# Where an S5 mixer's state coefficients are applied: to B before the scans, or to C between them

## The chip, the cores and the metric

The kernel runs on one core of a Trainium2 chip. The metric is the device time of one execution in microseconds. Three executions of the kernel before gave 1158.82, 1159.68 and 1162.73 us, a median of 1159.68 us.

## The reference

One decoder block over 256 tokens of width 1024, in float32. Cut to what matters here:

```python
h = modulate(rms_norm(x, g_mix), sh1, sc1)
u, q, k, v, ga, gb = split(h @ w_in)
# S5: 32 groups of 16 channels, 64 complex states per group
abar = exp(a * dt);  coef = (abar - 1) / a            # complex, one per group and state
bu   = einsum('bsgc,gpc->bsgp', u, coef[..., None] * b)   # bbar = coef * b
x_   = scan over positions: x_[t] = abar * x_[t-1] + bu[t]
y    = Re(einsum('gcp,bsgp->bsgc', c, x_)) + d_skip * u
y_a  = glu(gelu(y));  y_b = attention(q, k, v) @ w_attn_o     # 8 heads, causal, partial rotary
x    = x + gt1 * ((sigmoid(ga) * y_a + sigmoid(gb) * y_b) @ w_out)
h2   = modulate(rms_norm(x, g_ffn), sh2, sc2)
x    = x + gt2 * moe(h2)          # top 4 of 32 experts, each [1024 x 2048] and [1024 x 1024]
out  = rms_norm(x, g_final)
```

The coefficient `coef` of a state multiplies the state's input. The recurrence is linear, so the same factor may stand on the way out instead: Re(c · (coef · x')) = Re((c · coef) · x'), where x' is the scan of b·u without the coefficient.

## The kernel before, in words

Five engines run one program each, tied by semaphores. The order of each engine's work is written out by hand; no scheduler moves it. A first part (to about 250 us) computes the mixer, with the weights streamed from HBM through `ring`, 12 slots of 1 MB; the rest loops over the 32 experts, 12 MB of weights each, through four regions that the mixer has left (`zone` and `ring`). SyncE (SP) issues nearly all the loads in one order; `wait_free` and the waits on `w_used` hold a load back until TensorE has finished with the slot that it overwrites.

States are laid out as 16 columns of 128 (two groups of 64 states each). The eight *pairs* j cover two columns each. The steps of the S5 part are:

- The *phase tables* `ecos`, `esin` (cosine and sine of t times each state's angle) are built by doubling: VectorE (DVE) for the lower eight columns, GpSimd (POOL) for the upper eight (`square`, `double`, L320 to L325). The recurrence then runs on turned numbers and needs real scans only.
- *B*: `b_in` holds the 16 columns of B. DVE multiplies them by the coefficients (`sprm` 3 and 4, L1549 to L1551), ScalarE (ACT) spreads them into blocks with a mask (L1268, behind the negation of C's imaginary half, L1264), TensorE (PE) transposes the blocks (`b_columns`, L703), and ACT copies the result to `BT` (L1272).
- `b_u(j)` on PE (L678): four products of B with u for pair j, into PSUM banks 4 and 5. For j > 0 it waits until the scans of pair j-1 are done, since all pairs use the same two banks.
- `recurrence(j)` on DVE: six products and sums with the phase tables (L1585 to L1592) and four scans (L1597). Pair 0 to 7 in order.
- POOL turns the scans of pair j back, six operations of 128x512 (L1425 to L1430), into `xs`. All their operands lie in SBUF. From j = 2 on it waits for `xs_read`, the product `c_x(j/2 - 1)`.
- `c_x(m)` on PE (L693) multiplies C with four columns (two pairs) of `xs`; `skip(m)` on DVE (L1618) adds d·u.

These steps are interleaved with the projections (`proj`, L659 and L662) and with the attention of a pair of heads. The loop over p = 0 to 3 stands on PE as: `scores(p)` (L730, L734), first half of `proj(4+p)`, `c_x(p)`, `b_u(2p+3)`, a quarter of the projection, `probs_columns(p)` (L742), the last quarter, `weigh(p)` (L753), `b_u(2p+4)`. On DVE it stands as: `largest(p)` (L1604, waits for the scores), `recurrence(2p+2)`, `inverse_sums(p)`, `skip(p)`, `recurrence(2p+3)`. So `b_u(2p+3)` waits for `recurrence(2p+2)`, which stands behind `largest(p)`, which waits for `scores(p)`. Ahead of the loop DVE does `recurrence(0)`, `rotary(1)` (L1561 to L1564, all in SBUF), `recurrence(1)`.

After the loop come the attention's output projection (L830), the GLU products (L847), the output projection (L922, L949), the router, and the first expert. ACT asks for the router's and the biases' weights (L1284 to L1288, five loads in small packets) just ahead of the GELU (L1290) and two sigmoids (L1293, L1294).

## Time and profile before

| | |
|---|---|
| Median of three executions | 1159.68 us |
| The profiled execution's own time | 1159.92 us |
| Its span, first to last instruction | 1158.0 us |
| PE busy | 1122.6 us (97%) |
| DVE, ACT, POOL busy | 442.8, 140.9, 105.1 us |
| Granted TensorE clock, mean | 0.998 of full speed |
| Moved by DMA | 459.46 MB, mean 397 GB/s |

The span is cut into 40 slices of 29 us in the page's second part, a digit each for the busy share in tenths. Almost every slice has both PE and the DMA engines near full, so neither total says which of them sets the end in which stretch; the chain of waits and the stretches' own DMA shares do. POOL works only in the first five slices, where the S5 part lies. A busy figure of PE contains matmuls whose ends are modelled.

### The profile page before, as it was taken

How to read it: one execution, taken by the hardware profiler on the slowest of the kernel's cores; microseconds unless marked ns; L12 is line 12 of the kernel's file. 1: busy time of each engine (PE TensorE's matmuls, PEld its weight loads, DVE VectorE, ACT ScalarE, POOL GpSimd, SP SyncE). 2: the span in 40 equal slices, each digit the busy share in tenths (PEclk: the TensorE clock that was granted, in tenths of full speed). 3: DMA queues.
4: the chain of work that ended last, by engine and by line, in shares of the span. 5: the costliest groups of instructions: out<-in, count | busy, mean ns of one | idle time of the engine just before them, and what ended most of it. 6: DMA issues, size and time to landing. Idle time of an engine off the chain costs nothing.

```text
span 1158.0 us, 17087 instructions
## 1 busy us (share of the span) xinstructions
PE 1122.6 (97%) x6970; PEld 491.0 (42%) x6970; DVE 442.8 (38%) x952; ACT 140.9 (12%) x313; POOL 105.1 (9%) x142
## 2 busy tenths in 40 slices
PE   8999999999999999999999999999999999999996
PEld 6657788544333333333333333333333333333332
DVE  7857668263222333332222322222222222222224
ACT  3222240231000000000000000000000000000002
POOL 6496810000000000000000000000000000000000
PEclk9999999999999999999999999999999999999999
DMA  9983389999999999999999999999999999999994
GB/s 385 393 305 102 101 335 400 421 349 422 423 427 434 428 428 430 431 430 430 430 434 429 429 432 430 431 425 431 431 430 431 430 431 432 431 431 426 427 424 202
DMA packets 39839, 459.46 MB, mean 397 GB/s; under 512 B 3732, under 2 KB 4248, under 8 KB 16120
## 3 DMA queue, kind: packets, MB, share of 16 engines
q1 hardware_dynamic: 39088, 458.09, 94.3%
q10 hardware_dynamic: 712, 0.81, 0.2%
q8 instruction: 30, 0.49, 0.2%
q14 instruction: 9, 0.07, 0.0%
HBM read 457.83 MB, written 1.05 MB: 396 GB/s over the span
## 4 chain that ended last, share of the span: by engine, by line
PE 78%; DMA 18%; DVE 1%; ACT 1%; issue 1%; SPq 1%; DVEq 0%
PE ps L1086 30%; PE ps L1133 17%; DMA ring<-in_w_gu 16%; PE ps L662 5%; PE ps L1054 4%; PE ps L998 3%; PE ps L847 2%; PE ps L659 2%; PE ps L1110 2%; PE ps L865 2%; DMA ring<-in_first 1%; PE ps L830 1%; PE ps L922 1%; PE ps L623 1%; PE ps L629 1%; PE ps L1118 1%
## 5 line engine op out<-in xcount | busy, mean ns | idle before, releaser
L1086 PE MATMUL ps<-ring,zone 128*64 128x512 f32 x1024 | 227.0, 595 | 9.6 <-DMA ring<-in_w_gu 9.6
L1133 PE MATMUL ps<-ring,tmp 128*64 128x512 f32 x1012 | 224.2, 594 | 10.4 <-ACT tmp L1363 10.4
L1086 PE MATMUL ps<-zone 128*64 128x512 f32 x1024 | 227.2, 595 | 1.3 <-DMA zone<-in_w_gu 1.2
L1854 DVE TENSOR_TENSOR x_tok<-x_tok,ps 128x512 f32<-128x512 f32 x128 | 81.9, 681 | 261.4 <-PE ps L1054 260.1
L1086 PEld LDWEIGHTS ps<-ring,zone 128*64 128x64 f32 x1024 | 70.7, 137 | 161.6 <-issue 143.5
L1133 PEld LDWEIGHTS ps<-ring,tmp 128*64 128x64 f32 x1012 | 83.2, 137 | 130.7 <-issue 130.7
L1086 PEld LDWEIGHTS ps<-zone 128*64 128x64 f32 x1024 | 70.7, 137 | 154.1 <-issue 146.9
L1360 ACT ACTIVATE tmp<-hT 128x256 f32<-128x256 f32 x64 | 23.9, 417 | 722.8 <-DVE hT L1869 722.8
L1869 DVE TENSOR_SCALAR hT<-ps 128x256 f32<-128x256 f32 x64 | 24.2, 419 | 189.9 <-PE ps L1086 189.9
L1848 DVE TENSOR_TENSOR tmp<-ps,zone 128x512 f32<-128x512 f32 x32 | 22.1, 691 | 162.8 <-PE ps L1133 162.8
L1054 PE MATMUL ps<-tmp,xn_tok 64*128 64x512 f32 x248 | 70.0, 641 | 0.0
L662 PE MATMUL ps<-hT,ring 128*128 128x256 f32 x256 | 57.9, 382 | 0.0
L998 PEld LDWEIGHTS ps<-ptmp,zone 128*128 128x128 bf16 x1488 | 45.1, 98 | 23.6 <-issue 23.6
L662 PEld LDWEIGHTS ps<-hT,ring 128*128 128x128 f32 x256 | 47.7, 190 | 7.4 <-issue 1.4
L998 PE MATMUL ps<-ptmp,zone 128*128 128x64 bf16 x1488 | 48.8, 193 | 0.0
L1054 PEld LDWEIGHTS ps<-tmp,xn_tok 64*128 64x128 f32 x248 | 18.7, 184 | 50.3 <-issue 50.3
L865 PE MATMUL ps<-cst,ptmp 32*64 32x512 f32 x256 | 34.8, 613 | 0.0
L1041 PE MATMUL ps<-cst,ptmp 32*64 32x512 f32 x128 | 34.4, 613 | 0.0
L1110 PE MATMUL ps<-cst,ptmp 32*64 32x512 f32 x128 | 34.4, 613 | 0.0
L1363 ACT COPY tmp<-ps 128x256 f32<-128x256 f32 x64 | 20.8, 375 | 86.3 <-PE ps L1118 86.3
L659 PE MATMUL ps<-ring,hT 128*128 128x512 f32 x64 | 28.2, 594 | 0.0
L847 PE MATMUL ps<-zone,ring 128*128 128x256 f32 x128 | 28.2, 380 | 0.0
(339 smaller groups left out, 889.5 us busy)
## 6 DMA issues: line engine op xcount, KB each, us to landing
ring<-in_w_down SPq DMA_DIRECT2D x60, 2048.0 KB, 17.8
zone<-in_w_gu SPq DMA_DIRECT2D x23, 4096.0 KB, 26.9
ring<-in_w_gu SPq DMA_DIRECT2D x23, 4096.0 KB, 29.2
zone<-in_w_gu SPq DMA_DIRECT2D x14, 2048.0 KB, 13.1
ring<-in_w_gu SPq DMA_DIRECT2D x13, 2048.0 KB, 14.1
ring<-in_w_ada SPq DMA_DIRECT2D x16, 1024.0 KB, 13.1
ring<-in_w_in SPq DMA_DIRECT2D x12, 1024.0 KB, 14.6
ring<-in_w_gu SPq DMA_DIRECT2D x10, 1024.0 KB, 9.5
```

Of the source, the lines that this page charges most:

```text
L659: last = mm(ps[:, b + i, :], hT[:, k, P * i:P * i + P], w[:, kk, :], start=(k == 0), stop=(k == KD - 1))
L662: last = mm(ps[:, b + m // 2, (m % 2) * T:(m % 2) * T + T], w[:, kk, P * m:P * m + P], hT[:, k, :], start=(k == 0 and m % 2 == 0), stop=(k ...
L847: last = mm(ps[:, b + m // 2, (m % 2) * T:(m % 2) * T + T], w[:, kk, P * m:P * m + P], gluT[:, kk, :], start=(kk == 0 and m % 2 == 0), sto ...
L865: mm(ps[CAP * h:CAP * h + CAP, b, :], hotb[own, :], brow[own, 512 * h:512 * h + 512], start=True, stop=False, skip_group_check=True)
L998: last = mm(ps[:, 2, CAP * f:CAP * f + CAP], xpart[:, c, i, stored(f)], pick[:, i, :], start=(i == 0 and c == 0), stop=(i == TT - 1 and c ...
L1041: last = mm(ps[CAP * h:CAP * h + CAP, 5, :], hotb[3 * EXPERTS:P, :], brow[3 * EXPERTS:P, 0:2 * T], start=True, stop=True, skip_group_check ...
L1054: mm(ps[:, 6 + h, :], pickwT[half, P * t:P * t + P], ysb[half, :], start=True, stop=True).then_inc(S["comb_up"], 1)
L1086: last = mm(ps[CAP * h:CAP * h + CAP, b, :], hg[:, 2 * j + kk, :], w[:, kk, D * b + 512 * h:D * b + 512 * h + 512], start=False, stop=(j = ...
L1110: last = mm(ps[CAP * h:CAP * h + CAP, 3, :], hotb[own, :], brow[own, 512 * h:512 * h + 512], start=True, stop=False, skip_group_check=True)
L1133: last = mm(ps[CAP * h:CAP * h + CAP, 3, :], actT[:, q, j, :], row[:, 512 * h:512 * h + 512], start=False, stop=(j == DN_PIECES - 1 and q ...
L1854: V.tensor_tensor(x_tok[:, t, 512 * h:512 * h + 512], x_tok[:, t, 512 * h:512 * h + 512], ps[:, bank + h, :], ALU.add).then_inc(S["comb_ad ...
L1869: V.tensor_scalar(rows_of(gate[:, pair[g]]), down_pair(ps[:, 0, :], g), LIMIT, None, ALU.min).then_inc(S["gated"], 1)
```

## The change

B is no longer multiplied by the coefficients. The host lays B out in the transposed blocks, zeros included (512 KB instead of 256 KB), and one load brings them straight into `BT`. DVE's six operations on B, ACT's four spreads, PE's eight transposes and ACT's copy are gone. `weighted_c(m)` is new on DVE: six operations of 128x128 that multiply C's part m, in place, by the coefficients, with the negation of the imaginary half in the last one. Piece 0 stands behind `recurrence(1)`, pieces 1 to 3 behind `recurrence(3)`, `(5)` and `(7)`; `c_x(m)` waits for its piece. `b_u(0, 1)` does two pairs in one go, pair 1 into banks 6 and 7. The five late loads on ACT's queue are issued behind the GELU and the sigmoids.

```diff
--- before.py
+++ after.py
@@ -111,7 +111,12 @@
 
 def b_layout(b_re, b_im):
 
-    return np.concatenate([b[0].reshape(ST, 2, N, C).transpose(1, 2, 0, 3).reshape(P, ST * C) for b in (b_re, b_im)], axis=1)
+    out = np.zeros((4, 2, C, 2, KW, 2, N), np.float32)
+    for r, w in enumerate((b_re, b_im)):
+        w = w[0].reshape(KW, 4, 2, N, C)
+        for q in range(2):
+            out[:, q, :, r, :, q, :] = w[:, :, q].transpose(1, 3, 0, 2)
+    return out.reshape(P, 2 * KW * P)
 
 
 def c_layout(c_re, c_im):
@@ -218,18 +223,11 @@
     def stored(k):
         return slice(P * (2 * (k % RUN) + k // RUN), P * (2 * (k % RUN) + k // RUN) + P)
 
-    def b_sum(r):
-        return tmp[:, r, 0:T].rearrange("p (s c) -> p s c", s=ST)
-
-    b_in = kT.rearrange("p m t -> p (m t)")[:, 0:512].rearrange("p (r s c) -> p r s c", r=2, s=ST)
     work = gbT.rearrange("p m t -> p (m t)")[:, 0:10 * ST].rearrange("p (j s) -> p j s", s=ST)
     sprm = sb("sprm", [P, 5, ST])
 
     def state(j):
         return sprm[:, j, :] if j < 5 else work[:, j - 5, :]
-
-    blk = z.rearrange("p b r n -> p (b r n)")
-    Bblk = blk[:, 0:1024].rearrange("p (r s q c) -> p r s q c", r=2, s=ST, q=2)
 
     wide = 2048
     phases_at, mixer_at = (zone[:, 4 * wide * j:4 * wide * j + 4 * wide] for j in range(2))
@@ -374,6 +371,7 @@
 
     PROJ_BANK = (0, 2, 0, 2, 0, 0, 0, 4)
     TURN_BANK = (2, 0)
+    BU_BANK = (4, 6, 4, 4, 4, 4, 4, 4)
     MOD_BANK = {1: 6, 2: 2}
     LAST_BANK = (6, 0)
     GU_PIECES, DN_PIECES = 4, 2
@@ -459,7 +457,7 @@
             for n in range(place["uq", 3] + 1):
                 load_piece(n)
             sp.dma_start(cst[:, 0:C_ALL], const[:, :]).then_inc(S["const_in"], 16)
-            sp.dma_start(b_in.rearrange("p r s c -> p (r s c)"), b_laid[:, :]).then_inc(S["const_in"], 16)
+            sp.dma_start(BT.rearrange("p r m n -> p (r m n)"), b_laid[:, :]).then_inc(S["const_in"], 16)
             sp.dma_start(CT.rearrange("p r m n -> p (r m n)"), c_laid[:, :]).then_inc(S["const_in"], 16)
             for n in range(place["uq", 3] + 1, place["glu", 0]):
                 load_piece(n)
@@ -664,28 +662,27 @@
                 if part[-1] == 3 and ms[-1] == 3:
                     last.then_inc(w_used, 1)
 
-            def b_u(j):
-
-                if j == 0:
+            def b_u(*pairs):
+
+                if pairs[0] == 0:
                     pe.wait_ge(S["proj_sb"], 1)
-                    pe.wait_ge(S["BT_sb"], 1)
+                    pe.wait_ge(S["const_in"], 48)
                 else:
-                    pe.wait_ge(S["scanned"], 4 * j)
+                    pe.wait_ge(S["scanned"], 4 * pairs[0])
                 for r in range(2):
-                    for q in range(2):
-                        s = 2 * j + q
-                        a = 32 * (s % 4)
-                        last = mm(ps[:, 4 + q, T * r:T * r + T], BT[a:a + 32, r, s // 4, :], uT[a:a + 32, s // 4, :],
-                                  start=True, stop=True, skip_group_check=True)
-                last.then_inc(S["bu_up"], 1)
+                    for j in pairs:
+                        for q in range(2):
+                            s = 2 * j + q
+                            a = 32 * (s % 4)
+                            last = mm(ps[:, BU_BANK[j] + q, T * r:T * r + T], BT[a:a + 32, r, s // 4, :], uT[a:a + 32, s // 4, :],
+                                      start=True, stop=True, skip_group_check=True)
+                last.then_inc(S["bu_up"], len(pairs))
 
             def c_x(m):
 
                 pe.wait_ge(S["xs_set"], 2 * m + 2)
-                if m == 0:
-                    pe.wait_ge(S["const_in"], 48)
-                    pe.wait_ge(S["c_set"], 1)
-                else:
+                pe.wait_ge(S["c_set"], 2 * m + 2)
+                if m > 0:
                     pe.wait_ge(S["y_skip"], m)
                 for r in range(2):
                     for s in range(4):
@@ -693,16 +690,6 @@
                         last = mm(ps[a:a + 32, 6, (m % 2) * T:(m % 2) * T + T], CT[:, r, m, a:a + 32],
                                   xs[:, s // 2, r, T * (s % 2):T * (s % 2) + T], start=(r == 0), stop=(r == 1), skip_group_check=True)
                 last.then_inc(S["xs_read"], 1)
-
-            def b_columns():
-
-                pe.wait_ge(S["mod1_sb"], 4)
-                for r in range(2):
-                    pe.wait_ge(S["Bblk_set"], 2 * r + 2)
-                    for m in range(KW):
-                        last = nc.tensor.transpose(ps[:, 6 + r, P * m:P * m + P],
-                                                   Bblk[:, r, 4 * m:4 * m + 4].rearrange("p s q c -> p (s q c)"), ident)
-                last.then_inc(S["BT_up"], 1)
 
             def turned_columns(n):
 
@@ -767,13 +754,11 @@
             pair(0, 6), pair(0, 7)
             pair(1, 6), pair(1, 7)
             proj(2, 0)
-            b_columns()
             turned_columns(0)
             proj(2, 1, (0,))
-            b_u(0)
+            b_u(0, 1)
             proj(2, 1, (1, 2, 3))
             proj(3, 0)
-            b_u(1)
             turned_columns(1)
             proj(3, 1)
             for p in range(HEADS // 2):
@@ -1260,16 +1245,7 @@
                 nc.scalar.copy(oT[:, p, :], ps[:, 7, 0:T]).then_inc(S["o_sb"], 1)
 
             projected(0, uT)
-            act.wait_ge(S["const_in"], 48)
-            nc.scalar.activation(CT[:, 1], CT[:, 1], ACT.Copy, scale=-1.0).then_inc(S["c_set"], 1)
-            for r in range(2):
-                act.wait_ge(S["Bsum_set"], r + 1)
-                for q in range(2):
-                    nc.scalar.activation(Bblk[:, r, :, q, :], b_sum(r), ACT.Copy,
-                                         scale=cst[:, C_MB + q:C_MB + q + 1]).then_inc(S["Bblk_set"], 1)
             projected(1, q_tok)
-            act.wait_ge(S["BT_up"], 1)
-            nc.scalar.copy(BT[:, :, :, :].rearrange("p r m n -> p (r m n)"), ps[:, 6:8, :].rearrange("p b n -> p (b n)")).then_inc(S["BT_sb"], 1)
             turned(0)
             projected(2, k_tok)
             turned(1)
@@ -1281,17 +1257,17 @@
             head_pair(3)
             head_out(3)
             projected(7, gbT[:, 4:8, :])
+            act.wait_ge(S["y_skip"], KW)
+            nc.scalar.activation(gluT, uT, ACT.Gelu_apprx_tanh).then_inc(S["gelu"], 1)
+
+            act.wait_ge(S["proj_sb"], 8)
+            nc.scalar.activation(gbT, gbT, ACT.Sigmoid).then_inc(S["sig_gb"], 1)
+            nc.scalar.activation(gaT, gaT, ACT.Sigmoid).then_inc(S["sig_ga"], 1)
             act.dma_start(wr.rearrange("p (a b) e -> p a (b e)", b=RUN), w_router[0].rearrange("(a p b) e -> p a (b e)", p=P, b=RUN)).then_inc(S["late_in"], 16)
             act.dma_start(brt[:, :], b_router.to_broadcast([P, EXPERTS])).then_inc(S["late_in"], 16)
             for j in range(2):
                 act.dma_start(brow[EXPERTS * j:EXPERTS * j + EXPERTS, :], b_gu[0, :, D * j:D * j + D]).then_inc(S["late_in"], 16)
             act.dma_start(brow[2 * EXPERTS:3 * EXPERTS, :], b_down[0]).then_inc(S["late_in"], 16)
-            act.wait_ge(S["y_skip"], KW)
-            nc.scalar.activation(gluT, uT, ACT.Gelu_apprx_tanh).then_inc(S["gelu"], 1)
-
-            act.wait_ge(S["proj_sb"], 8)
-            nc.scalar.activation(gbT, gbT, ACT.Sigmoid).then_inc(S["sig_gb"], 1)
-            nc.scalar.activation(gaT, gaT, ACT.Sigmoid).then_inc(S["sig_ga"], 1)
 
             def row_copy(n):
 
@@ -1541,15 +1517,21 @@
                 level(n)
             square(V, link, T // 2, LOW)
 
-            dve.wait_ge(S["const_in"], 48)
-            cr = sprm[:, 3, :].unsqueeze(2).to_broadcast([P, ST, C])
-            ci = sprm[:, 4, :].unsqueeze(2).to_broadcast([P, ST, C])
-            t0, t1 = (tmp[:, j, T:2 * T].rearrange("p (s c) -> p s c", s=ST) for j in range(2))
-            for r in range(2):
-                link(V.tensor_tensor(t0, b_in[:, r], cr, ALU.mult))
-                link(V.tensor_tensor(t1, b_in[:, 1 - r], ci, ALU.mult))
-                V.tensor_tensor(b_sum(r), t0, t1, ALU.subtract if r == 0 else ALU.add).then_inc(S["Bsum_set"], 1)
-                dve.wait_ge(S["Bsum_set"], r + 1)
+            def weighted_c(m):
+
+                if m == 0:
+                    dve.wait_ge(S["const_in"], 48)
+                cr, ci = (sprm[:, j, 4 * m:4 * m + 4].unsqueeze(2).to_broadcast([P, 4, 2 * C]) for j in (3, 4))
+                c0, c1 = (CT[:, r, m].rearrange("p (s c) -> p s c", s=4) for r in range(2))
+                t0, t1 = (tmp[:, r, 0:P].rearrange("p (s c) -> p s c", s=4) for r in range(2))
+                link(V.tensor_tensor(t0, c1, ci, ALU.mult))
+                link(V.tensor_tensor(t1, c0, ci, ALU.mult))
+                link(V.tensor_tensor(c0, c0, cr, ALU.mult))
+                link(V.tensor_tensor(c1, c1, cr, ALU.mult))
+                V.tensor_tensor(c0, c0, t0, ALU.subtract).then_inc(S["c_set"], 1)
+                V.scalar_tensor_tensor(c1, t1, -1.0, c1, ALU.mult, ALU.subtract).then_inc(S["c_set"], 1)
+                dve.wait_ge(S["c_set"], 2 * m + 2)
+
             def rotary(n):
 
                 heads = (q_tok, k_tok)[n].rearrange("p i (h d) -> p i h d", d=HD)[:, :, :, 0:2 * HALF]
@@ -1565,7 +1547,7 @@
                 dve.wait_ge(S["rotated"], n + 1)
 
             double(V, link, T // 2, slice(0, ST // 4), (ptmp, probs))
-            dve.wait_ge(S["Bblk_set"], 4)
+            dve.wait_ge(S["const_in"], 48)
             rotary(0)
             double(V, link, T // 2, slice(ST // 4, ST // 2), (ptmp, probs))
             V.engine_nop().then_inc(S["phases"], 1)
@@ -1574,7 +1556,7 @@
 
                 b = j % 2
                 cs, sn = ecos[:, 2 * j:2 * j + 2, :], esin[:, 2 * j:2 * j + 2, :]
-                br, bi = (ps[:, 4:6, T * r:T * r + T] for r in range(2))
+                br, bi = (ps[:, BU_BANK[j]:BU_BANK[j] + 2, T * r:T * r + T] for r in range(2))
                 t0, t1 = (tmp[:, r, :].rearrange("p (s t) -> p s t", s=2) for r in range(2))
                 zz = [z[:, b, r, :].rearrange("p (s t) -> p s t", s=2) for r in range(2)]
                 dve.wait_ge(S["bu_up"], j + 1)
@@ -1647,6 +1629,7 @@
             recurrence(0)
             rotary(1)
             recurrence(1)
+            weighted_c(0)
             for p in range(HEADS // 2):
                 largest(p)
                 if 2 * p + 2 < 8:
@@ -1655,6 +1638,7 @@
                 skip(p)
                 if 2 * p + 3 < 8:
                     recurrence(2 * p + 3)
+                    weighted_c(p + 1)
 
             def attended(h):
```

Left out above are the two lines that name semaphores. Where the rows of an engine's program move is seen best on DVE, at the start of the loop. Before, behind `rotary(1)` (L1561 to L1564):

```order
L1564 TENSOR_TENSOR zone<-zone,tmp 128x16x16
L1585 TENSOR_TENSOR tmp<-ps,zone 128x512
L1586 TENSOR_TENSOR tmp<-ps,zone 128x512
L1588 TENSOR_TENSOR ps<-ps,zone 128x2x256
L1589 TENSOR_TENSOR ps<-ps,zone 128x2x256
L1591 TENSOR_TENSOR ps<-tmp,ps 128x2x256
L1592 TENSOR_TENSOR ps<-tmp,ps 128x2x256
L1597 SCALAR_TENSOR_TENSOR zone<-sprm,ps 128x256 x4
L1604 TENSOR_REDUCE mx<-ps 128x2
```

The last row is `largest(0)`. After, the same place, from the scans of `recurrence(1)` on:

```order
L1579 SCALAR_TENSOR_TENSOR zone<-sprm,ps 128x256 x4
L1527 TENSOR_TENSOR tmp<-zone,sprm 128x128
L1528 TENSOR_TENSOR tmp<-zone,sprm 128x128
L1529 TENSOR_TENSOR zone<-zone,sprm 128x128
L1530 TENSOR_TENSOR zone<-zone,sprm 128x128
L1531 TENSOR_TENSOR zone<-zone,tmp 128x128
L1532 SCALAR_TENSOR_TENSOR zone<-tmp,zone 128x128
L1586 TENSOR_REDUCE mx<-ps 128x2
```

Six rows now stand between the scans and the reduction; the same six stand at three further places. On PE, before, from the first half of `proj(2)` (L659) on, with `b_columns` (L703), `turned_columns` (L714) and `b_u` (L678):

```order
L659 MATMUL ps<-ring,hT 128x512 x8
L703 MATMUL ps<-head,zone 128x128 x8
L714 MATMUL ps<-head,zone 128x128 x8
L659 MATMUL ps<-ring,hT 128x512 x2
L678 MATMUL ps<-zone 128x256 x4
L659 MATMUL ps<-ring,hT 128x512 x14
L678 MATMUL ps<-zone 128x256 x4
L714 MATMUL ps<-head,zone 128x128 x8
```

After, where L701 is `turned_columns` and L677 is `b_u`:

```order
L657 MATMUL ps<-ring,hT 128x512 x8
L701 MATMUL ps<-head,zone 128x128 x8
L657 MATMUL ps<-ring,hT 128x512 x2
L677 MATMUL ps<-zone 128x256 x8
L657 MATMUL ps<-ring,hT 128x512 x14
L701 MATMUL ps<-head,zone 128x128 x8
```

The eight transposes are gone, and the four products of pair 1 stand with those of pair 0.

## Rows read from the trace of the kernel before

**Rows 1.** PE's waits from 60 to 252 us: total, times, longest.
```profile
PE ps L960 <- DVE zone L1764: 0.2, 1, 0.2
PE ps L1086 <- DVE zone L1787: 0.2, 1, 0.2
```
**Rows 2.** Stretches: length; PE, PEld, DVE, ACT, POOL busy; clock, DMA share, GB/s.
```profile
160.00:226.00 66.00, 65.90 (x301) 48.59 (x301) 41.89 (x31) 14.22 (x15) 0.00 (x0) 1.00 1.01 403
231.00:235.00 4.00, 4.00 (x24) 1.77 (x20) 3.11 (x11) 0.00 (x0) 0.00 (x0) 1.00 0.62 199
300.00:820.00 520.00, 513.97 (x3198) 186.04 (x3196) 149.99 (x346) 33.91 (x90) 0.00 (x0) 1.00 1.01 430
820.00:1129.00 309.00, 294.64 (x1860) 107.16 (x1858) 89.05 (x208) 20.72 (x55) 0.00 (x0) 1.00 1.00 429
```
**Rows 3.** The chain that ended last: start, length, what.
```profile
824.36 7.10 PE ps L1133 x32
...
832.82 36.13 DMA ring<-in_w_gu
```
**Rows 4.** PE's timeline: start, us, line, op, output<-inputs, shape, count.
```profile
50.70 7.03 PE L659 MATMUL ps<-ring,hT 128*128 128x512 f32 x16
57.57 1.04 PE L703 MATMUL ps<-head,zone 128*128 128x128 f32 x8
58.44 1.04 PE L714 MATMUL ps<-head,zone 128*128 128x128 f32 x8
...
113.65 1.13 PE L678 MATMUL ps<-zone 32*128 32x256 f32 x8
...
151.26 1.07 PE L693 MATMUL ps<-zone 128*32 128x256 f32 x16
```
**Rows 5.** DVE's timeline: largest(0); then from the scans of pair 3 to those of pair 4.
```profile
85.87 0.42 DVE L1604 TENSOR_REDUCE mx<-ps 128x2 f32<-128x256 f32 x1 [3.95 <-PE ps L734]
...
98.77 2.41 DVE L1597 TENSOR_TENSOR_SCAN zone<-sprm,ps 128x256 f32<-128x256 f32 x4
105.71 0.42 DVE L1604 TENSOR_REDUCE mx<-ps 128x2 f32<-128x256 f32 x1 [4.53 <-PE ps L734]
...
107.34 0.68 DVE L1585 TENSOR_TENSOR tmp<-ps,zone 128x512 f32<-128x512 f32 x1
...
111.18 2.41 DVE L1597 TENSOR_TENSOR_SCAN zone<-sprm,ps 128x256 f32<-128x256 f32 x4
```
**Rows 6.** DVE's timeline: rotary(1), four operations.
```profile
68.69 0.29 DVE L1561 TENSOR_TENSOR tmp<-zone,cst 128x128 f32<-128x128 f32 x1
69.02 1.02 DVE L1562 TENSOR_TENSOR tmp<-zone,cst 128x128 f32<-128x128 f32 x1
70.07 1.22 DVE L1563 TENSOR_TENSOR zone<-zone,cst 128x256 f32<-128x256 f32 x1
71.32 1.36 DVE L1564 TENSOR_TENSOR zone<-zone,tmp 128x256 f32<-128x256 f32 x1
```
**Rows 7.** POOL's timeline: the tables beside rotary(1), then pairs 0, 2, 3 and 7.
```profile
68.85 1.04 POOL L323 TENSOR_TENSOR zone<-zone 128x508 f32<-128x508 f32 x1
...
71.09 1.32 POOL L325 TENSOR_TENSOR zone<-zone 128x508 f32<-128x508 f32 x1
...
79.79 1.26 POOL L1430 TENSOR_TENSOR zone<-zone,ptmp 128x512 f32<-128x512 f32 x1
...
94.00 1.27 POOL L1425 TENSOR_TENSOR zone<-zone 128x512 f32<-128x512 f32 x1 [3.93 <-PE ps L693]
...
102.10 1.27 POOL L1425 TENSOR_TENSOR zone<-zone 128x512 f32<-128x512 f32 x1
...
148.58 1.27 POOL L1430 TENSOR_TENSOR zone<-zone,ptmp 128x512 f32<-128x512 f32 x1
```
**Rows 8.** ACT's timeline: the first row behind the late loads.
```profile
163.37 1.28 ACT L1290 ACT_TABLE_LOAD   x1 [1.14 <-issue]
```

**Rows 9.** Load issued from 15 to 19 us: queue, count, size, us to landing.
```profile
ring<-in_w_in SPq DMA_DIRECT2D x1, 1024.0 KB, 26.2
```

More of the change, by code:

```diff
@@ L279, in build @@
     shift_set = sem("shift_set")
-    names = """x_in const_in head_in late_in gfin_in out_stored ones_set cond_set sprm_sb Bblk_set
-        BT_up BT_sb c_set phases modrow_sb modT_up mod1_sb sq1 xn1 xT_up
+    names = """x_in const_in head_in late_in gfin_in out_stored ones_set cond_set sprm_sb c_set phases modrow_sb modT_up mod1_sb sq1 xn1 xT_up
         hD_sb hA_sb proj_sb bu_up scanned xs_set xs_read rotated turned_up turned_sb sc_up negmax expd probs
@@ L288, in build @@
         x_split scale1_set turn turned row_max sqsum2 lnD lnA lnP
-        cond_half u_up biased_scale ada_used Bsum_set mask_set phase_hi scale2_set hgl_up hgl_sb sums_set""".split()
+        cond_half u_up biased_scale ada_used mask_set phase_hi scale2_set hgl_up hgl_sb sums_set""".split()
     S = {n: sem(n) for n in names}
```

## The prediction

> **What bounds the kernel now.** I read the chain of waits first. Up to 824 us it is TensorE's own products with a few tenths of a microsecond between them; behind that it steps on to the weight loads [rows 3]. The DMA engines are full in both stretches, 430 and 429 GB/s at a share of 1.01 and 1.00 [rows 2]: from about 256 us on one saturated stream carries the experts' weights, and TensorE first works ahead of its end and is then caught by it. So the end moves with the moment at which that stream starts. What starts it is TensorE: from 160 to 226 us the loads run at 403 GB/s, but from 231 to 235 us they fall to 199 (share 0.62) [rows 2], because every load that may be issued has landed and the next waits for slots that TensorE frees. Whatever was gained or lost in loading before that is forgotten there. TensorE in turn waits 0.4 us in all between 60 and 252 us [rows 1]. The conclusion for the sum: a microsecond more or less on TensorE between 50 and 230 us is a microsecond at the end, and the DMA side gives nothing back.
>
> The second reading is of who is nearly late for TensorE. In the loop over head pairs the DVE idles only ahead of `largest`: 3.95 us in round 0, 4.53 us in round 1, until the scores arrive [rows 5]; round 2 repeats round 1 instruction by instruction, and I count it as equal. From there it has no air. The scans of pair 4 end at 111.18 + 2.41 = 113.59 us [rows 5], and `b_u(5)`, which waits for them, starts at 113.65 us [rows 4]. TensorE and DVE run neck and neck, with a slack that I put at 0.1 us. Any time by which `largest` starts late beyond that is a stall of TensorE at `b_u(2p+3)`.
>
> **The change part by part.** The sum is made against the profiled execution, 1159.92 us (span 1158.0), which lies 0.24 us above the median of 1159.68.
>
> *Transposes gone.* The eight of `b_columns` hold TensorE from 57.57 to 58.44 us, where the next begins [rows 4]: -0.87 us, all on the path.
>
> *DVE's, ACT's work on B gone, BT's copy gone.* These end before `rotary(0)`, which waits for q's projection, and TensorE is in an unbroken product from 50.70 us on until the transposes [rows 4]. Nothing waits for them: 0. The floor is 0 as well, since no wait of TensorE has them as its releaser [rows 1].
>
> *Larger B.* 256 KB more at about 400 GB/s is 0.65 us for the loads behind it. The first of these, asked for after 16 us, lands 26.2 us later [rows 9], about 43 us; its first use is at 50.70 us [rows 4]. Hidden with 7 us to spare; without that cover it would cost 0.65.
>
> *Two pairs at once.* `b_u(1)`'s four products (1.1 us, as those of `b_u(5)` [rows 4]) move forward from behind `proj(3, 0)` to `b_u(0)`. No work is added. `recurrence(0)` starts 1.1 - 0.87 = 0.2 us later, `recurrence(1)` no longer waits for TensorE and starts some 2 to 3 us sooner. That gives DVE room ahead of `largest(0)` and nothing to TensorE: 0.
>
> *Late weights.* ACT reaches the GELU's table at 163.37 us, 1.14 us of it idle for the issues [rows 8]. The five issues go behind the GELU and the sigmoids, some 5 us later. Neither ACT nor the loads are waited for by TensorE there [rows 1], and the stream is reset at 231 us anyway: 0, at most 0.5 either way if small packets meet a weight that is wanted. The cover is the distance to the router, which stands behind the GLU and half of the output projection on TensorE; without it TensorE would wait for the landing of the last small load, by those same 5 us at most.
>
> *Coefficients on C: the term that decides.* Each piece is six DVE operations of 128x128, each fed from two SBUF operands. Alone, such an operation takes 0.29 us ([rows 6], L1561), and six with their semaphore steps take 6 x 0.33 = 2.0 us, well inside 4.53 us of idle time. But they do not run alone. POOL works on six operations of 1.27 us per pair with starts 8.10 / 6 = 1.35 us apart (94.00 to 102.10), and goes on with pair 3 at once [rows 7]. The trace holds one place where DVE operations with two SBUF operands meet long POOL operations: `rotary(1)`. There a 128x128 operation takes 1.02 us and the two next 1.22 and 1.36 [rows 6], instead of 0.29 and 0.42. The ends tell why: the second ends at 70.04, POOL's operation at 69.89; the last ends at 72.68, POOL's at 72.41 [rows 6, 7]. DVE gets one operation through per POOL operation, just behind its end.
>
> So a piece costs by POOL's rhythm. Scans of pair 2p+3 end while the last operation of pair 2p+2 runs on POOL (pair 3's scans end at 101.18, POOL's operation at 102.0); the first operation of the piece waits some 0.6 us and takes 0.15, the five others 1.35 each: 7.5 us. Bounds: 2.0 us without any meeting; 7.0 to 8.2 by the phase in which the first one hits; 8.8 if POOL is held back as long as DVE works, (1.27 + 0.29 + 0.03) x 5 + 0.8. I take 7.5, as the rotary rows are the same kind of work.
>
> Price: in rounds 1 and 2 `largest` starts 7.5 - 4.53 = 2.97 us late, less 0.1 slack, a stall of 2.87 us each at `b_u(5)` and `b_u(7)`: +5.7. Once stalled, every product behind is late by the same, so the next round's idle time is again 4.53 and the stall repeats. For round 0, `rotary(1)` is done at 72.9 to 74.0 us (its first operation slips in ahead of POOL's at 68.85 or not), `recurrence(1)` (113.59 - 107.34 = 6.25 us [rows 5]) at 79.2 to 80.4; the six operations then follow POOL's ends from 79.79 + 1.26 on [rows 7] and are done at 86.6 to 87.9. TensorE's scores are there at 85.87 - 0.87 = 85.0 [rows 5]: a stall of 1.4 to 2.8 us, I take 2.1. Round 3 has no `b_u` behind `largest`; what follows are the probabilities, wanted behind `c_x(3)` (151.26 + 1.07 us [rows 4]) and a quarter of a projection. Late by 3 us they would still be there: 0, at most 1 if not.
>
> Sum: -0.87 + 2.1 + 5.7 = +7.0 us. 1159.92 + 7.0 - 0.24 gives about 1166.7 us as a median. Its own range: pieces of 7.0 to 8.2 us give -0.87 + 1.4 + 4.8 = +5.3 to -0.87 + 2.8 + 7.2 = +9.1, or 1165 to 1169.
>
> Does POOL slow down too? Its operation beside the last of `rotary(1)` took 1.32 us, against 1.27 for the slightly wider ones of pair 2 with DVE's operations out of its way [rows 7]: +0.05, so six cost 0.3 us. `c_x(3)` starts at 151.26 us [rows 4] and POOL's last ends at 149.85 [rows 7], a slack of 1.4: nothing. The Trainium skill (SBUF — State Buffer, Who interferes with whom) says that a DVE instruction with two SBUF inputs and a GpSimd one that reads SBUF take a shared port by an exclusive lock, and that the one that comes second fully blocks. For DVE's side the rotary rows agree. For POOL's side it would be 6 x 0.29 = 1.7 us per piece, more than the slack of 1.4, and the time would go to the upper case below; the row of 1.32 us speaks for much less.
>
> **The rivals.**
>
> *No meeting: the pieces hide (not slower).* If a 128x128 piece ran at 0.33 us per operation, it would fill 2.0 of 4.53 idle microseconds and only the transposes would count: -0.9, 1158.8 us. It decides as soon as a piece takes under 4.6 us. For it: the idle time is there, and L1561 did take 0.29. Against it: L1562 to L1564, three of three that started under a POOL operation.
>
> *Half a meeting.* The last two operations of a piece are not tied by a wait, and may pass in one gap of POOL. Then a piece takes 6.15 us; stalls are 1.5, 1.5 and about 0.8, the sum is +3.0 and the time 1162.7 us. For it: no wait of the program stands between the two. Against it: POOL's next operation begins 1.35 - 1.27 = 0.08 us behind its last [rows 7] and would come between.
>
> *POOL is held back as well.* Pieces of 8.8 us: 4.2 us in rounds 1 and 2, 3.3 in round 0, and `c_x(3)` late by 0.3: -0.9 + 3.3 + 8.4 + 0.3 = +11.1, 1170.8 us.
>
> **How the numbers follow.** The forecast, pieces at POOL's rhythm: 0.58. Half a meeting: 0.15. No meeting: 0.15. POOL held back: 0.08. Something that the rows do not show and that makes it faster than the sum allows: 0.04. A measurement of this kernel tells about 0.3% (3.5 us) from no change. Slower by more than that, above 1163.2 us, are the forecast and the upper case, less a small tail: 0.64. Within it are no meeting and half a meeting: 0.32. Faster: 0.04. The time is that of the forecast. The range from 1158.5 to 1169.5 us takes in the forecast and both lower cases and leaves out the upper one and the last.
>
> **What would show it.** In the profile after: the operations of `weighted_c` at a mean near 1.2 us instead of 0.3, each ending just behind a POOL operation; DVE without idle time ahead of `largest` in rounds 1 and 2; a wait of TensorE at `b_u` for the scans, three times, near 2, 2.9 and 2.9 us; POOL's operations near 1.3 us; then the same sequence as before up to the end, shifted by the sum. It is wrong if the operations take 0.3 us; if they take 1.2 but TensorE shows no wait, then my slack of 0.1 us was misread; if TensorE stalls but the span does not grow by as much, the stream of weights had air that I did not see, and the share in the dip at the end of the mixer would show it.

## The result, and the profile after

The changed kernel takes 1162.37 us (median of 20 executions, 1160.81 to 1164.63), the kernel before, on the same chips, 1160.08 us (20 executions, 1158.56 to 1162.73). The ratio is 1.0020 with a 95% interval of 1.0014 to 1.0025: slower by 2.3 us. The forecast was 1166.7 us, a rise of 7.0 us over the median of three: the sign is right, the size three times too large. The profiled execution took 1164.63 us, its span is 1162.8 us.

The page after, part 1 (busy time, share of the span, instructions): DVE has 22 us more work, POOL 0.6 us, TensorE no more.

```profile
PE 1122.3 (97%) x6962; PEld 490.2 (42%) x6962; DVE 464.8 (40%) x970; ACT 137.9 (12%) x307; POOL 105.7 (9%) x142
```

The waits of TensorE from 60 to 252 us, which answer to [rows 1] (total, times, longest):

```profile
PE ps L677 <- DVE zone L1579: 4.1, 3, 1.4
PE ps L945 <- DVE zone L1748: 0.2, 1, 0.2
```

Three waits for the scans (L1579), at `b_u` (now L677), are new. The timeline of TensorE shows each (start, duration, what, and in brackets the idle time ahead and its releaser); it answers to [rows 4]:

```profile
60.33 1.15 PE L677 MATMUL ps<-zone 32*128 32x256 f32 x16
92.99 1.13 PE L677 MATMUL ps<-zone 32*128 32x256 f32 x8 [1.19 <-DVE zone L1579]
...
114.34 1.13 PE L677 MATMUL ps<-zone 32*128 32x256 f32 x8 [1.45 <-DVE zone L1579]
115.40 3.72 PE L660 MATMUL ps<-hT,ring 128*128 128x256 f32 x16
...
135.67 1.13 PE L677 MATMUL ps<-zone 32*128 32x256 f32 x8 [1.42 <-DVE zone L1579]
136.73 5.41 PE L660 MATMUL ps<-hT,ring 128*128 128x256 f32 x16
...
164.69 14.08 PE L815 MATMUL ps<-zone,ring 128*128 128x256 f32 x64
```

(TensorE's rows count each of these float32 products twice: x8 is one pair's four, x16 is eight.) Two things here stood in no forecast. `b_u(0, 1)`, twice the work, takes 1.15 us, as long as one pair's (1.13). And the 16 products behind the third wait take 5.41 us, where those behind the second take 3.72. The stretches show why, and answer to [rows 2] (busy time of PE, PEld, DVE, ACT, POOL, granted clock, DMA share, GB/s):

```profile
136.70:142.00 5.30, 5.30 (x19) 4.30 (x18) 5.08 (x9) 0.51 (x2) 4.99 (x5) 0.68 0.14 56
231.00:235.00 4.00, 4.00 (x40) 2.04 (x38) 0.48 (x2) 2.65 (x3) 0.00 (x0) 1.00 1.01 420
235.00:240.00 5.00, 5.00 (x23) 2.25 (x20) 4.40 (x12) 0.00 (x0) 0.00 (x0) 1.00 0.68 241
820.00:1129.00 309.00, 294.10 (x1862) 106.91 (x1860) 89.13 (x207) 20.72 (x55) 0.00 (x0) 1.00 1.00 430
```

The granted clock is 0.68 from 136.70 to 142.00 us: part of the time at 1.2 instead of 2.4 GHz, behind three stretches in which TensorE idled (1.19, 1.45 and 1.42 us). The loads' dip has moved with TensorE, from 231 us to 235 us and later, and behind it the stream runs at 430 GB/s as before: nothing was given back.

DVE in round 1, answering to [rows 5]:

```profile
100.36 0.88 DVE L1527 TENSOR_TENSOR tmp<-zone,sprm 128x128 f32<-128x128 f32 x1
101.27 1.31 DVE L1528 TENSOR_TENSOR tmp<-zone,sprm 128x128 f32<-128x128 f32 x1
102.62 1.31 DVE L1529 TENSOR_TENSOR zone<-zone,sprm 128x128 f32<-128x128 f32 x1
103.96 1.31 DVE L1530 TENSOR_TENSOR zone<-zone,sprm 128x128 f32<-128x128 f32 x1
105.31 1.31 DVE L1531 TENSOR_TENSOR zone<-zone,tmp 128x128 f32<-128x128 f32 x1
106.54 0.28 DVE L1532 SCALAR_TENSOR_TENSOR zone<-tmp,zone 128x128 f32<-128x128 f32 x1
106.85 0.42 DVE L1586 TENSOR_REDUCE mx<-ps 128x2 f32<-128x256 f32 x1
107.19 0.68 DVE L1587 TENSOR_REDUCE mx<-ps 128x2 f32<-128x512 f32 x1
107.91 0.17 DVE L1589 TENSOR_SCALAR mx<-mx 128x4 f32<-128x4 f32 x1
```

and POOL beside it, answering to [rows 7]:

```profile
103.86 1.27 POOL L1403 TENSOR_TENSOR zone<-zone,ptmp 128x512 f32<-128x512 f32 x1
105.20 1.27 POOL L1404 TENSOR_TENSOR zone<-zone 128x512 f32<-128x512 f32 x1
106.55 1.39 POOL L1405 TENSOR_TENSOR ptmp<-zone 128x512 f32<-128x512 f32 x1
```

Five operations each end just behind one of POOL's; the sixth starts in the same gap as the fifth and takes 0.28 us. POOL's operation beside it takes 1.39 instead of 1.27 us (spans on POOL are rough). The piece is 6.46 us long (100.36 to 106.82). And a third surprise: `largest` ends with a small operation (L1589) of 0.17 us, where the kernel before has (its timeline of DVE, behind the row of 105.71 us in [rows 5]):

```profile
106.05 0.68 DVE L1605 TENSOR_REDUCE mx<-ps 128x2 f32<-128x512 f32 x1
106.76 0.66 DVE L1607 TENSOR_SCALAR mx<-mx 128x4 f32<-128x4 f32 x1
```

**Where the time went.** One measure serves for all kernels below: the *segment*, from the start of `proj(2, 0)` (50.70 us before, 50.78 after) to the start of the attention's output projection (160.82 and 164.69). It is 110.12 us before and 113.91 after: +3.8. Of this the transposes make -0.87, `b_u(1)` for nothing -1.1, the three waits +4.1 and the lowered clock +1.7 (5.41 - 3.72), in sum +3.8. From there to the last products ahead of the first expert it is 85.74 and 85.57 us. That makes 3.7 of the 4.8 us by which the profiled span grew; the other 1.1 us lie in the experts' loop, where the change has no code. From those products to the last 32 of the last expert it is 893.66 us before and 894.75 after, and 892.3 to 895.0 in all thirteen traces, so a single execution's total says little about a microsecond. Ahead of the segment TensorE waits for its first loads, 0.6 to 2.5 us in all, and the segment starts at 50.69 to 51.63 us.

### The profile page after: what moved, and what is told of

It is laid out like the page before. It is cut to its first block, busy times and chain, and to the rows that moved or that the text cites. A ratio compares the mean times of both kernels' runs of the same rounds, so it can differ in the third digit from the quotient of the medians.

```text
span 1162.8 us, 17085 instructions
## 1 busy us (share of the span) xinstructions
PE 1122.3 (97%) x6962; PEld 490.2 (42%) x6962; DVE 464.8 (40%) x970; ACT 137.9 (12%) x307; POOL 105.7 (9%) x142
## 4 chain that ended last, share of the span: by engine, by line
PE 71%; DMA 19%; DVE 7%; issue 1%; ACT 1%; SPq 0%; DVEq 0%
PE ps L1071 28%; DMA ring<-in_w_gu 16%; PE ps L1118 16%; PE ps L1039 4%; PE ps L983 3%; PE ps L832 2%; PE ps L1095 2%; DMA ring<-in_w_down 2%; PE ps L660 2%; PE ps L850 2%; PE ps L621 1%; PE ps L815 1%; PE ps L657 1%; PE ps L907 1%; PE ps L627 1%; DVE zone L1579 1%
```

## The experiments

Eleven kernels ran, all variants of the changed one, in three groups, each beside its own executions of the kernel before (32, 19 and 23, with medians of 1160.10, 1160.41 and 1160.50 us). Every ratio is against the group's own. The theory after the result: pieces are slow because of two SBUF operands beside POOL, an untied last operation shares a gap, `b_u(1)` is free because its products use other rows of the array than those of `b_u(0)`. The rival of the first: the time is that of the place in the program, whatever stands there.

**early**: all of C weighted in six operations of 128x512 ahead of `rotary(0)`, where DVE waits for q's projection; everything else as changed.

```diff
-            dve.wait_ge(S["const_in"], 48)
+            all_c()
             rotary(0)
...
-            weighted_c(0)
...
-                    weighted_c(p + 1)
```

> All of C is weighted at once, six operations of 128x512, ahead of rotary(0), where POOL is idle and DVE has 2.8 us of removed work and 2.7 us of idle time. Theory (pieces run at POOL's rhythm, and that alone cost time): the six take 6 x 0.72 = 4.3 us, no wait of TensorE at b_u for the scans over 0.2 us, TensorE reaches the attention's output projection at 160.82 - 0.87 - 1.1 = 158.8 us, time about 1158.0 us, ratio to before 0.998. Rival (the bigger B, the moved b_u or the late loads cost the time): the ratio stays at 1.002.

1158.27 us, ratio to before 0.9981 (0.9972 to 0.9990). No wait at `b_u`; the segment is 108.06 us. DVE there:

```profile
46.10 0.69 DVE L1526 TENSOR_TENSOR tmp<-zone,sprm 128x512 f32<-128x512 f32 x1
...
49.61 0.69 DVE L1531 SCALAR_TENSOR_TENSOR zone<-tmp,zone 128x512 f32<-128x512 f32 x1
52.87 0.29 DVE L1542 TENSOR_TENSOR tmp<-zone,cst 128x128 f32<-128x128 f32 x1 [2.58 <-ACT zone L1220]
...
105.55 0.67 DVE L1588 TENSOR_SCALAR mx<-mx 128x4 f32<-128x4 f32 x1
```

The 4.2 us of work end 2.58 us before `rotary(0)` may start: they cost nothing. The small operation of `largest` takes 0.67 us again, so the change in it belongs to the pieces. By the ratio this version beats the kernel before, by 1.8 us, and so the changed one too.

**early_split**: the same, with `b_u(0)` and `b_u(1)` apart at their old places.

```diff
-            b_u(0, 1)
+            b_u(0)
             proj(2, 1, (1, 2, 3))
             proj(3, 0)
+            b_u(1)
```

> As the one with C weighted early, but b_u(0) and b_u(1) stand apart, at their places of the kernel before. Theory (eight products of two pairs use four groups of 32 rows side by side and so take no longer than four of one pair): TensorE is 1.1 us later than in the other at the output projection, 159.9 us; time 1159.1 us. Rival (the 1.1 us came from a wait that went, not from the products): the two kernels reach it within 0.2 us of each other.

1158.66 us, 0.9988 (0.9979 to 0.9997); the segment is 109.25 us, 1.19 longer than early's. Joining the pairs is worth 1.2 us in the segment (the medians differ by 0.4 only, which is within their noise), and the transposes' 0.87 is confirmed: 110.12 - 109.25.

**dummy_sbuf** and **dummy_psum**: early, and at the pieces' places six operations of the same shapes whose results nobody uses; their second operand lies in SBUF in the one and in PSUM in the other.

```diff
+                link(V.tensor_tensor(t0, c1, ci, ALU.mult))
+                link(V.tensor_tensor(t1, c0, ci, ALU.mult))
...
+            piece(0)
...
+                    piece(p + 1)
```

and in dummy_psum, against dummy_sbuf:

```diff
+                other = ps[:, 6, half:half + P].rearrange("p (s c) -> p s c", s=4)
-                link(V.tensor_tensor(t0, c1, ci, ALU.mult))
+                link(V.tensor_tensor(t0, c1, other, ALU.mult))
...
```

> C is weighted early, and four further pieces stand where the changed kernel has its own, the same six operations with the same two SBUF operands, results thrown away. Theory: mean over a piece's operations 1.1 us, piece 6.5 us, TensorE waits three times, 4.1 us in all, time 4.1 us above the early one, about 1162. Rival (the cost was in c_x waiting for C, not in DVE's time): no waits, as the early one.

> The same four further pieces, but the second operand of each operation comes from a PSUM bank instead of SBUF. Theory (two SBUF operands make an operation wait for POOL's): 0.29 us per operation, piece 2.0 us, inside 4.5 us of idle time, no wait of TensorE, time as the early one, 1158.0. Rival (six operations with their semaphore steps cost that much whatever POOL does): piece 6.5 us and 4.1 us of waits as with SBUF operands.

With SBUF: 1162.42 us, 1.0021 (1.0011 to 1.0032), the segment 112.15. With PSUM: 1158.06 us, 0.9985 (0.9975 to 0.9994), the segment 108.05, early's to 0.01. The waits of TensorE and two of DVE's rows in dummy_sbuf, then DVE's rows in dummy_psum:

```profile
PE ps L677 <- DVE zone L1591: 4.0, 3, 1.4
```

```profile
101.88 1.31 DVE L1540 TENSOR_TENSOR tmp<-zone,sprm 128x128 f32<-128x128 f32 x1
...
107.14 0.28 DVE L1544 SCALAR_TENSOR_TENSOR tmp<-tmp 128x128 f32<-128x128 f32 x1
```

```profile
99.70 0.26 DVE L1541 TENSOR_TENSOR tmp<-zone,ps 128x128 f32<-128x128 f32 x1
100.00 0.29 DVE L1542 TENSOR_TENSOR tmp<-zone,ps 128x128 f32<-128x128 f32 x1
...
101.17 0.28 DVE L1546 SCALAR_TENSOR_TENSOR tmp<-tmp,ps 128x128 f32<-128x128 f32 x1
104.38 0.42 DVE L1600 TENSOR_REDUCE mx<-ps 128x2 f32<-128x256 f32 x1 [2.93 <-PE ps L721]
```

Six operations in the same place cost 4.1 us of the segment or nothing, by where one operand lies. The rival of the place falls. `c_x` waits for these pieces too, but TensorE shows no wait there.

**six_tied**: the changed kernel, with a wait between the last two operations of a piece.

```diff
                 V.tensor_tensor(c0, c0, t0, ALU.subtract).then_inc(S["c_set"], 1)
+                dve.wait_ge(S["c_set"], 2 * m + 1)
```

> The changed kernel with one wait more in each piece, between the last two operations. Theory (an untied neighbour passes in the same gap of POOL, a tied one needs a gap of its own, 1.35 us): piece 7.8 us instead of 6.5, TensorE's three waits 2.6 to 2.8 us each instead of 1.2 to 1.5, time 4.0 us above the changed kernel, about 1166. Rival (the last operation of a piece is fast because of its kind, scalar_tensor_tensor, and not because nothing ties it): it stays at 0.3 us and the time does not move.

1167.82 us (four executions), 1.0075 (1.0054 to 1.0095). The last two operations:

```profile
107.07 1.31 DVE L1531 TENSOR_TENSOR zone<-zone,tmp 128x128 f32<-128x128 f32 x1
108.42 1.31 DVE L1533 SCALAR_TENSOR_TENSOR zone<-tmp,zone 128x128 f32<-128x128 f32 x1
```

The piece is 7.6 us long (102.15 to 109.73), the waits 2.33, 2.56 and 0.90 us: the forecast's model, had its premise held. The third wait is short, and the clock is 0.72 from 117 to 123 us; I read it as the slower products having delayed the scores and taken part of the wait's place. The segment is 115.60 us, 1.7 longer than the changed kernel's. The time rose by more than that and than the 4.0 expected (5.1 us, each kernel against its own group); with four executions that stays open.

**pair_by_pair**: `b_u(0, 1)` with the loop over pairs outermost.

```diff
-                for r in range(2):
-                    for j in pairs:
+                for j in pairs:
+                    for r in range(2):
```

> The changed kernel with the products of b_u(0, 1) written pair by pair instead of alternating between the pairs. Theory (the 1.1 us came from four row groups in neighbouring products at work at once): b_u(0, 1) takes 2.2 us instead of 1.1, time 1.1 us above the changed kernel. Rival (it came from issuing eight products in one go behind one wait): stays at 1.1 us.

The expectation missed: the eight products take 1.16 us (61.16 to 62.25, where the next begins: 1.09), not 2.2. 1163.17 us, 1.0021 (1.0011 to 1.0030). The order in which row groups are used does not matter here.

**same_rows** (one execution): early_split with `b_u(0)`'s four products doubled, all eight in rows 0 to 63.

```diff
+                            if j == 0:
+                                last = mm(ps[:, 6 + q, T * r:T * r + T], BT[a:a + 32, r, 1, :], uT[a:a + 32, 1, :],
```

> C weighted early, b_u(0) and b_u(1) apart, and each of pair 0's four products issued with a neighbour that uses the same 32 rows and writes bank 6 or 7 (overwritten later). Eight products behind one wait, in rows 0 to 63 alone. Theory (eight products take no longer than four only where they use four row groups): the eight take 2.0 us, TensorE 1 us later than without the neighbours. Rival (the saving comes from eight products being issued in one go): 1.1 us.

```profile
61.11 0.71 PE L677 MATMUL ps<-zone 32*128 32x256 f32 x4
61.65 0.60 PE L680 MATMUL ps<-zone 32*128 32x256 f32 x4
62.08 0.70 PE L677 MATMUL ps<-zone 32*128 32x256 f32 x4
62.51 0.70 PE L680 MATMUL ps<-zone 32*128 32x256 f32 x4
63.14 1.13 PE L657 MATMUL ps<-ring,hT 128*128 128x512 f32 x2
```

Eight products take 2.03 us in two row groups; in the changed kernel eight in four groups take 1.08 (60.33 to 61.41). The segment is 110.21 us, 0.96 longer than early_split's. Eight products in one go are not enough; the other rows make the gain.

**late_back** and **early_late_back**: the five late loads back ahead of the GELU, in the changed kernel and in early.

```diff
...
+            act.dma_start(brt[:, :], b_router.to_broadcast([P, EXPERTS])).then_inc(S["late_in"], 16)
...
             act.wait_ge(S["y_skip"], KW)
             nc.scalar.activation(gluT, uT, ACT.Gelu_apprx_tanh).then_inc(S["gelu"], 1)
```

> The changed kernel with the five late loads back ahead of the GELU. Theory: neither place is waited for, the time stays within 0.5 us of the changed kernel's, and TensorE's products from the attention's output projection to the first expert take as long. Rival (small packets behind other loads cost the weight stream time at the new place): 1 to 2 us less than the changed kernel.

> C weighted early, pairs together, and the five late loads back ahead of the GELU. Theory (the place of the late loads is worth nothing; what the changed kernel with them moved back showed beyond 0.6 us of waiting was the spread of the granted clock's drops): within 0.3 us of the one with C weighted early, 1158.2, TensorE's stretch from the attention's output projection to the first expert 85.6 us. Rival (the old place delays DVE's sums and TensorE waits 0.6 us at L784): 0.6 us more.

Both expectations missed. late_back: 1163.99 us, 1.0033 (1.0021 to 1.0045), 1.3 us more than the changed kernel when each is taken against its own group (the intervals of the two ratios overlap, so the size is uncertain); TensorE waits 0.60 us at L784 and the part behind the segment is 0.67 us longer. early_late_back: 1159.61 us, 0.9993 (0.9981 to 1.0004), by the groups 0.9 above early, with intervals that overlap as well. TensorE in it, and DVE in it and in early:

```profile
174.32 1.06 PE L784 MATMUL ps<-zone,ones 128*32 128x512 f32 x8 [0.95 <-issue]
```

```profile
168.34 1.23 DVE L1644 TENSOR_TENSOR zone<-ps,zone 128x1024 f32<-128x1024 f32 x1 [3.87 <-ACT zone L1269]
```

```profile
166.93 1.22 DVE L1644 TENSOR_TENSOR zone<-ps,zone 128x1024 f32<-128x1024 f32 x1 [2.12 <-PE ps L815]
```

With the issues ahead, GELU and sigmoids are late, DVE waits for the sigmoid instead of for TensorE, its product with it (L1644) is late by 1.4 us and so are the modulation's sums behind that (L1624), and the products of L784, which need these sums, wait 0.95. In the kernel before, which issues at that place too, the segment is 2 us longer, which hides all but 0.17 us (85.74 against 85.57).

**dummy_four** (one execution, 1159.05 us): early with four tied SBUF operations at the pieces' places.

```diff
+                link(V.tensor_tensor(d0, c0, cr, ALU.mult))
+                V.tensor_tensor(d1, c1, cr, ALU.mult).then_inc(S["c_set"], 2)
```

> C weighted early, and four further pieces at the changed kernel's places with four tied operations instead of six, two SBUF operands each, results thrown away. Theory (one operation per POOL operation; largest may be late by 0.5 us before TensorE waits, because the small operation behind it then falls into a gap of POOL): piece 0.9 + 3 x 1.35 = 4.9 us, 0.4 us more than the idle time, and no wait of TensorE at b_u over 0.1 us. Rival (any lateness passes to TensorE): waits of 0.4 us in rounds 1 and 2.

The piece is 5.1 us long, more than the 4.53 of idle time, and yet no wait of TensorE appears; the segment is 108.12. The slack ahead of `b_u` is 0.5 us or more, not 0.1, once a piece stands there.

**untied**: the changed kernel, whose pieces wait only where an operand needs it.

```diff
+                V.tensor_tensor(t0, c1, ci, ALU.mult).then_inc(S["w_set"], 1)
+                V.tensor_tensor(t1, c0, ci, ALU.mult).then_inc(S["w_set"], 1)
+                dve.wait_ge(S["w_set"], 4 * m + 2)
```

> The changed kernel, but in each piece DVE waits only where an operation reads or overwrites what another wrote: three untied couples instead of four tied operations and one couple. Theory (an untied neighbour shares a gap of POOL): piece 0.9 + 2 x 1.35 + 3 x 0.25 = 4.3 us, inside the 4.53 us of idle time plus 0.5, no wait of TensorE at b_u, no drop of the granted clock, time as with C weighted early, 1.9 us under the kernel before, 1158.2. Rival (only the last operation of a piece is fast): piece 6.5 us, waits of 4.1 us, time 1162.4.

```profile
99.60 0.99 DVE L1527 TENSOR_TENSOR tmp<-zone,sprm 128x128 f32<-128x128 f32 x1
100.52 0.28 DVE L1528 TENSOR_TENSOR tmp<-zone,sprm 128x128 f32<-128x128 f32 x1
100.83 1.25 DVE L1530 TENSOR_TENSOR zone<-zone,sprm 128x128 f32<-128x128 f32 x1
102.00 0.28 DVE L1531 TENSOR_TENSOR zone<-zone,sprm 128x128 f32<-128x128 f32 x1
102.31 1.24 DVE L1533 TENSOR_TENSOR zone<-zone,tmp 128x128 f32<-128x128 f32 x1
103.47 0.28 DVE L1534 SCALAR_TENSOR_TENSOR zone<-tmp,zone 128x128 f32<-128x128 f32 x1
104.28 0.42 DVE L1588 TENSOR_REDUCE mx<-ps 128x2 f32<-128x256 f32 x1 [0.53 <-PE ps L721]
...
105.34 0.91 DVE L1591 TENSOR_SCALAR mx<-mx 128x4 f32<-128x4 f32 x1
```

1158.38 us, 0.9986 (0.9976 to 0.9995). Two operations per gap of POOL, 4.15 us for the piece, and the small operation of `largest` now takes 0.91, beside POOL. DVE still idles 0.53 us ahead of `largest`, so it is this operation that leaves waits of 0.6 us in all; the segment is 108.75. The pieces may stay where they are; the waits inside them made the change slow. Against early the 0.1 us of the medians says nothing.

## Why the prediction was right or wrong

**What bounds the kernel: right.** The waits on TensorE went into the segment in full, the dip of the loads moved with it (from 231 us to 235), and nothing came back behind it.

**Transposes, -0.87: right** (early_split, 0.87). **DVE's and ACT's work on B, the larger B, 0: right**; no wait of TensorE in any trace has one of them as its releaser. The waits for the first loads are longer in the variants (0.7 to 2.5 us) than in the one trace of the kernel before (0.6); whether the larger B has a part in that is not shown, but early and dummy_psum gain 1.8 and 2.0 us by the medians and 2.1 by the segment, which leaves 0.2 us or less for it.

**Coefficients on C, +7.8: the step that failed.** The mechanism was right: DVE's operations with two SBUF operands get through at POOL's rhythm (1.31 us each), the dummies show that the operand's place is the cause, and three waits appear at `b_u`. Two sizes were off.
- The piece: 7.5 us assumed that the untied last operation finds POOL's next one in its way. It does not, 0.28 us in the same gap, and the piece takes 6.46. That was the second rival, "half a meeting", to which I gave 0.15: its piece was 6.15, its waits 1.5, 1.5 and 0.8, its time 1162.7 us. Measured: 1.45, 1.42, 1.19 and 1162.4. Its mechanism was right, but that its time came so near is partly luck: it left out the joined pairs (-1.1) and the clock. My reason against it was the gap of 0.08 us. POOL's next operation does begin 0.08 us behind its last (106.55), but it does not keep the sixth out; it takes 1.39 us itself. six_tied with 7.6 us shows the forecast's case.
- The slack: 0.1 us was read from a row of the kernel before in which the last operation of `largest` lost 0.5 us to POOL. With a piece ahead of it, it falls into POOL's gap and takes 0.17 instead of 0.66. `largest` starts 6.46 - 4.53 = 1.9 us late, TensorE waits 1.45; in dummy_four, where it starts 0.5 late, TensorE does not wait. Of the error of 1.4 us in each of rounds 1 and 2, 1.0 is the piece and the rest this. In round 0 the piece takes 6.5 us instead of 7.5 (1.19 of wait instead of 2.1).

The Trainium skill (SBUF — State Buffer, Who interferes with whom) also names the small operation: a `tensor_scalar` may enter a mode that uses both ports and contends with GpSimd. The trace agrees with 0.66, 0.67 and 0.91 us beside POOL and 0.17 in its gap; I had weighed the Trainium skill for the pieces alone. That the second one to come is blocked for the whole of the other's instruction is not seen on POOL's side, which gave 0.12 us for a DVE operation of 0.28 (spans on POOL are rough).

**Two pairs at once, 0: wrong by 1.1 to 1.2.** I counted the four products as moved with their time. They run in rows 64 to 127 beside the others in rows 0 to 63 (same_rows: 2.03 us when kept in two groups). The Trainium skill (TensorE: Matmul & The Clock Gate, Part 3: Packing small matmuls — row/col tiling) states that products of 32 rows in different row groups run at once, with 3.07x for four. Here four groups do in 1.08 us what two do in 2.03, a factor of 1.9 for twice the groups, so the trace agrees that they run at once; no run here has all in one group, so none tests the 3.07. I had the rows `32x256` before me and did not use them.

**Late weights, 0: nearly, and for a wrong reason.** No wait of TensorE in the kernel before named ACT, but the part behind its segment is 0.17 us longer than the changed kernel's, so ACT was at the limit already; its path goes over the sigmoid and DVE's sums. With a shorter way to this point, the old place costs 0.60 us of waiting in late_back and 0.95 in early_late_back. I looked for who is waited for, not for who is nearly late behind it.

**Not in the sum: the granted clock, +1.7.** In four of the five profiled kernels with waits of 1.2 us or more at `b_u`, the clock falls behind one of them (the changed kernel 0.68, six_tied 0.72, pair_by_pair and late_back below). In dummy_sbuf it does not, and in the mixer of the eight others it does not either:

```profile
136.00:144.00 8.00, 7.54 (x33) 0.79 0.27 113
```

```profile
114.00:126.00 12.00, 11.59 (x56) 0.86 0.21 81
```

(pair_by_pair and late_back; the span of time, TensorE's busy time, its granted clock, DMA share, GB/s.) Where it falls ahead of the third wait, it takes that wait's place: in late_back the third wait is gone, and its segment of 112.40 us is only 0.25 longer than that of dummy_sbuf, whose clock does not fall. Behind the third wait, as in the profile of the changed kernel, a fall costs its 1.7 us in full.

How often it falls is told only in part: each execution's mean clock is on record, but not where it fell. The mean is 0.997 or less in 16 of 20 executions of the changed kernel and in 19 of 74 of the kernel before. It can also fall at the kernel's end: in early and pair_by_pair the last expert's 32 products take 8.73 and 8.79 us instead of 7.09. So half or more of the changed kernel's executions seem to have a fall that the kernel before lacks. The sum of the terms without the clock, -0.87 - 1.1 + 4.1 = +2.1, is near the medians' +2.3 all the same. That would fit falls that mostly come ahead of the third wait, but no run shows it, and what the clock adds to the median stays open.

The sum as it should have been, the clock left out: -0.87 - 1.1 + 1.19 + 1.45 + 1.42 = +2.1 us, or 1162.2.

## What to carry to other kernels

DVE work with two SBUF operands beside a long chain of GpSimd operations cost one gap for each operation that was tied to the one before, and one for two that were not: drop the waits inside it that no operand needs, take one operand from PSUM, or put it where GpSimd is idle or DVE waits anyway. Read slack from a row only after asking what in the row itself is stretched by a neighbour. When products of few rows are moved next to each other, look whether they use the same rows of the array before counting their time twice.

## What the runs showed of the hardware

- A DVE operation of 128x128 with two SBUF operands that is not tied to the one before passes in the same gap of POOL: 0.28 us instead of 1.31 (the changed kernel against six_tied), and POOL's operation grows from 1.27 to 1.39 us. Untied pairs bring a piece of six from 6.5 to 4.15 us.
- The same six operations with one operand in PSUM run at 0.26 to 0.29 us beside the same POOL work (dummy_psum).
- A `tensor_scalar` of four elements, SBUF to SBUF, takes 0.17 us in POOL's gap and up to 0.91 beside its operation (untied).
- Eight float32 products of 32 rows take 1.08 us in four row groups (1.09 in the other order) and 2.03 us in two (same_rows).
- In four of the five traces with TensorE waits of 1.2 to 2.6 us in the loop, one of the waits was followed by some microseconds at a lowered clock (0.68 over 5.3 us, 0.72 over 6, 0.79 over 8, 0.86 over 12), about 1.7 us of clock each time.
